# Hybrid decoder trunk: input projection as three fp32r products of parts, and a convolution by channel blocks

## The chip, the cores and the metric

The kernel runs on one core of a Trainium2 chip. The metric is the device time of one execution in microseconds, the median of the runs shown.

## What is computed

Two layers are applied to 576 tokens: a prompt of 512 (positions 0 to 511) and 8 sample sequences of 8 tokens. All arrays are float32, the model width is 1024. Each layer:

```python
a = rmsnorm(h, w['norm_mix'][i])
zaq, zaf, zai, zag, zbqkv, zbg, zbb, zba, zc, zd = split_in(a @ w['w_in'][i])
oA, sa = mixer_hgrn2(...)      # gated linear recurrence
oB, sb, bb = mixer_gdn(...)    # gated delta rule, after a causal 4-tap convolution
oC, bc = mixer_conformer(...)  # below
oD, bd = mixer_pool(...)       # means over windows of 2, 4, 8, 16 tokens
h += concat[oA | oB | oC | oD] @ W_out
h += PEER(rmsnorm(h))          # 8 heads, top 16 of 128 x 128 experts
h += sigmoid(rmsnorm(h) @ W_gate) * (p[i] @ W_ple)
```

The two parts that the change touches are the product `a @ w_in` and the depthwise convolution of the conformer mixer, 31 taps over 256 channels:

```python
a, b = jnp.split(zc, 2, axis=-1)
u = a * jax.nn.sigmoid(b)
y, new_buf = causal_dwconv(u, buf, dw_w)      # 31 taps
y = jax.nn.silu(layernorm(y + dw_b, ln_g, ln_b))
```

## The kernel before

Each engine has its own hand-written program (`@block.tensor`, `@block.scalar`, `@block.gpsimd`, `@block.vector`, `@block.sync`), and its instructions run in the order in which they are written; `at(label)` gives the semaphore value at which a named step is done. So each engine's queue is a list, and what stands behind a waiting instruction waits too.

At the start of a layer `rms` (ACT), `scale` (DVE), `turn` (PE) and `turned` (DVE, line 2197) put the normalised tokens transposed into XT, 128 features by 576 tokens for each of 8 blocks k; five token tiles i, the last being the samples. The input projection then makes 20 feature tiles of 128 output columns (`FM`, line 101): ca0, cb0, ca1, cb1 for the convolution, p0, p1 for the pooling, f0, f1, q0, q1, then k0 to k5, ga0, ga1, gb0, gb1. A tile is done in two halves of 288 tokens, "p" and "s", 8 float32 products each (`feature_half`, line 829), so that the first halves can begin before the last tokens are there; the trace shows each float32 product as two records. Its weights, 512 KB, come into a ring of three buffers WF, loaded by SyncE when the tile three before it is done (line 655). After tiles 0 to 9 comes a token-major tile of 264 columns ("zt", line 880). Tiles 10 to 19 are mixed with other work of the mixers on PE.

ACT drains each half (`take`, line 1595), except ca0 and ca1: their drain is the gate on DVE (line 2268), which multiplies the PSUM half with the sigmoid into CU. When both channel blocks c are gated, DVE runs the convolution: for each of the 31 taps j, for both blocks c, one instruction for the 512 prompt tokens and one for the 64 sample tokens:

```python
for j in range(CCONV):
    for c in range(2):
        ...
        dve.did(STT(out, src, w, out, ALU.mult, ALU.add) ...)   # line 2282
    dve.wait_ge(dve_done, count("dve_done"))
```

Behind it stand, in DVE's queue, the pooling sums (lines 2297 to 2309), the forget gate (2318 to 2321), the scans (2333), the convolution's mean and variance (2345, 2360), and the memset of HSP (2373), after which POOL zeroes QP and KLOW (2056, 2057) and ACT copies into QP (1680). Then the score loop: 16 units u of the HGRN2 mixer. DVE makes the exponent's argument (`decay_steps`, 2390), ACT the exponentials (`unit_exp`, 1687 and 1688), POOL `k_low` (2066), DVE `q_low` (2400), PE the scores (`pair_scores`, 921), and DVE chooses them (`chosen`, 2412); every second unit DVE also runs one block of the 4-tap convolution (`conv`, 2448). PE does one feature tile per two units.

The later query projection (`query_half`, line 1339) is already written as three products of parts: a high part is an ACT copy into fp32r, a low part is a subtraction.

Of the kernel before, what the change touches and what calls it, by code (L numbers as in the profile page):

```python
# [23 lines left out]
D = 1024  # L24
# [168 lines left out]
def trunk(nc, din, dout, gates_dram, gelus_dram, known):  # L193
# [145 lines left out]
    AM = region(RING, 4, 128)  # L339
    place["at"] = QR_AT  # L340
# [99 lines left out]
    phase.close()  # L440

# [364 lines left out]
    def _(eng):  # L806
        pe = Engine(eng, "pe_done", counts)
        mm = eng.matmul

# [53 lines left out]
        for L in range(DEPTH):  # L863
# [10 lines left out]
            pe.wait_ge(sem("wt_loaded"), at("wt", L))  # L874
            for i in range(NT):
# [3 lines left out]
                for k in range(KT):  # L879
                    ins = mm(b[0:R, 0:TMW], XT[:, k, COL[i]:COL[i] + R], WT[:, k, :], start=(k == 0), stop=(k == KT - 1))  # L880
# [447 lines left out]
            PARTS = ((0, 0), (1, 0), (0, 1))  # L1328

# [224 lines left out]
    def _(eng):  # L1554
# [71 lines left out]

        act.wait_ge(sem("const_loaded"), at("consts"))
        for L in range(DEPTH):
            if L == 0:
                for i in range(NT):  # L1630
                    rms(0, i)
            if L:

                act.wait_ge(dve_done, at("lbx", L))
                act.did(A(LBV[:, 6:10], LBV[:, 6:10], ACT.Exp).then_inc(act_done, 1), "lbe", L)
            for j in range(FM_FIRST):
                take(L, j)
            for i in range(NT):
# [12 lines left out]
            take(L, FM_FIRST)  # L1651
            act.wait_ge(dve_done, at("cyc", L))
# [7 lines left out]
            take(L, FM_FIRST + 1)  # L1660
            act.wait_ge(dve_done, at("hla", L))
# [368 lines left out]
            sigmoid(3, 0)  # L2030
            sigmoid(3, 1)
            rms(3 * L + 3, 3)
            sigmoid(SAMPLE, 0)
            sigmoid(SAMPLE, 1)
            rms(3 * L + 3, SAMPLE)


    @block.gpsimd
    def _(eng):
        pool = Engine(eng, "pool_done", counts)  # L2040

        for L in range(DEPTH):

            if L:
                pool.wait_ge(dve_done, at("ple_done", L - 1))
# [9 lines left out]
            pool.wait_ge(dve_done, at("temps_free", L))  # L2055
# [122 lines left out]
    def _(eng):  # L2178
# [48 lines left out]

        dve.wait_ge(sem("const_loaded"), at("consts"))
        dve.wait_ge(sem("params_loaded"), at("params", 0))
        lg = par("logits")  # L2230
        for L in range(DEPTH):
            if L == 0:
                for i in range(NT):
                    scale(0, i)
                    if i:
                        turned(0, i - 1)
            turned(3 * L, NT - 1)

# [21 lines left out]
            for c in range(2):  # L2260
# [8 lines left out]
                counts.same(("cu_ready", L, c), ("drained", "z", L, ja, "s"))  # L2269
            for c in range(2):  # L2270
                dve.wait_ge(sem(f"cu{c}_loaded"), at("cu", L, c))
            dve.wait_ge(dve_done, count("dve_done"))

            for j in range(CCONV):
                for c in range(2):
                    w = par("cconv")[:, c * CCONV + j:c * CCONV + j + 1]
                    for out, src in ((CY[:, c, 0:SEQ], CU[:, c, j:j + SEQ]),
# [743 lines left out]
```

## Time and profile before

| | |
|---|---|
| median of 3 runs | 3974.62 us |
| the runs | 3991.79, 3974.62, 3974.47 us |
| span of the profiled execution | 3986.0 us |
| its mean granted TensorE clock | 0.981 of full speed |
| busy: PE, DVE, ACT, POOL | 3860.7, 2869.4, 1527.8, 2356.9 us |

The profiled execution's own time isn't listed apart; the span lies between two of the runs, so only the run of 3991.79 us can be its. Busy time is the time in which an engine executes. "Idle before" is the gap on the engine ahead of an instruction, with what ended it. PE is the matmul side of TensorE, PEld its weight loads.

### The profile page before, as it was taken

The page shows a single profiled execution, that of the slowest core. Times are in us where ns is not written, and L with a number is a line of the kernel's source. Part 1 is how long each engine was busy: PE and PEld are TensorE (multiplying, and loading weights), DVE is VectorE, ACT ScalarE, POOL GpSimd, SP SyncE. Part 2 cuts the span into 40 slices and gives each one's busy share as a digit, 9 for nine tenths or more (in the row PEclk, how much of TensorE's full clock was granted, in tenths as well). Part 3 has the DMA queues.
Part 4 walks back from the last instruction along what each step waited for, and adds up shares of the span by engine and source line. Part 5 has one row for each costly group of instructions (what it writes and reads, how often), then busy time and mean ns, then how long its engine had stood idle before and what let it go on. Part 6 is the DMA issues. An engine that isn't in the chain of part 4 may idle for free.

```text
span 3986.0 us, 59450 instructions
## 1 busy us (share of the span) xinstructions
PE 3860.7 (97%) x23204; PEld 3451.3 (87%) x23204; DVE 2869.4 (72%) x4845; ACT 1527.8 (38%) x2347; POOL 2356.9 (59%) x1456
## 2 busy tenths in 40 slices
PE   8999999999999999999999999999999999999999
PEld 6788699998999999999477876999999999999994
DVE  5765369945888778888467642799458887788875
ACT  1443255543333343333314422555433333343333
POOL 0131088887777568888101410888877774788881
PEclk9989999999999999999999889999999999999999
DMA  4201156666989999999221021566579999999992
GB/s 122 53 13 70 48 184 214 214 218 232 313 308 324 339 347 367 384 371 350 86 66 40 13 75 53 187 223 209 206 252 321 312 322 334 351 376 379 375 321 71
DMA packets 417976, 900.99 MB, mean 226 GB/s; under 512 B 94497, under 2 KB 242209, under 8 KB 416033
## 3 DMA queue, kind: packets, MB, share of 16 engines
q1 hardware_dynamic: 272288, 552.91, 40.6%
q0 software_dynamic: 90112, 268.76, 18.7%
q10 hardware_dynamic: 55296, 75.52, 5.2%
q8 instruction: 184, 3.01, 0.3%
q14 instruction: 96, 0.78, 0.1%
HBM read 773.87 MB, written 123.15 MB: 225 GB/s over the span
## 4 chain that ended last, share of the span: by engine, by line
PE 50%; POOL 23%; DVE 12%; DMA 7%; issue 6%; ACT 2%; DVEq 0%; SPq 0%; ACTq 0%; POOLq 0%
PE banks L1410 14%; POOL peer_gates L2128 10%; POOL u_stage L2144 9%; PE banks L839 7%; PE banks L1422 6%; PE banks L1519 4%; POOL u_stage L2136 3%; DMA peer_gates<-peer_v,u_stage 3%; PE banks L1321 3%; PE banks L1339 3%; DMA u_stage<-peer_ut 2%; DVE normed L2796 2%; PE banks L1484 2%; PE banks L1465 1%; DMA normed<-peer_ut 1%
## 5 line engine op out<-in xcount | busy, mean ns | idle before, releaser
L2128 POOL DMA_INDIRECT peer_gates<-peer_v,u_stage x512 | 778.7, 1521 | 323.7 <-DVE normed L2796 151.9
L1484 PE MATMUL banks<-gated_parts,v_parts 128*128 128x320 f32 x6144 | 916.1, 310 | 44.3 <-DVE gated_parts L2843 33.8
L1484 PEld LDWEIGHTS banks<-gated_parts,v_parts 128*128 128x128 f32 x6144 | 904.1, 188 | 56.6 <-issue 55.8
L1410 PE MATMUL banks<-peer_x_parts,u_parts 128*128 128x448 f32 x3168 | 662.9, 367 | 0.0
L1410 PEld LDWEIGHTS banks<-peer_x_parts,u_parts 128*128 128x128 f32 x3168 | 591.0, 188 | 44.8
L2144 POOL DMA_INDIRECT u_stage<-dense_gelus,u_stage x256 | 418.9, 1636 | 103.8 <-issue 77.4
L2812 DVE SCALAR_TENSOR_TENSOR peer_gates<-peer_gates,u_stage 128x1024 f32<-128x1024 f32 x254 | 326.0, 1283 | 150.0 <-DMA peer_gates<-peer_v,u_stage 138.1
L1410 PE MATMUL banks<-peer_x_parts,low_s 128*128 128x448 f32 x1696 | 397.7, 367 | 0.0
L2796 DVE SCALAR_TENSOR_TENSOR normed<-peer_gates,u_stage,normed 128x1024 f32<-128x1024 f32 x254 | 327.6, 1290 | 89.3 <-DMA peer_gates<-peer_v,u_stage 62.5
L1915 ACT ACTIVATE u_stage<-banks 128x448 f32<-128x448 f32 x256 | 139.2, 544 | 633.5 <-PE banks L1410 506.8
L2121 POOL TENSOR_TENSOR parts_a<-x,parts_a 128x1024 fp32r<-128x1024 f32 x64 | 170.2, 2679 | 358.2 <-ACT parts_a L1864 358.2
L2136 POOL DMA_INDIRECT u_stage<-gelus,u_stage x256 | 332.2, 1298 | 78.2 <-issue 78.0
L1410 PEld LDWEIGHTS banks<-peer_x_parts,low_s 128*128 128x128 f32 x1696 | 317.3, 188 | 23.5
L1991 ACT ACTIVATE gated_parts<-gated 128x320 fp32r<-128x320 f32 x256 | 120.8, 472 | 562.7 <-DVE gated L2833 402.1
L2835 DVE TENSOR_TENSOR v_parts<-v_stage,v_parts 128x1024 fp32r<-128x1024 f32 x256 | 312.0, 1219 | 15.6 <-ACT v_parts L1989 11.0
L839 PE MATMUL banks<-x,mixers 128*128 128x288 f32 x1280 | 316.2, 408 | 1.3 <-DVE kept L2240 0.7
L839 PEld LDWEIGHTS banks<-x,mixers 128*128 128x128 f32 x1280 | 242.0, 190 | 68.3 <-issue 1.1
L1989 ACT ACTIVATE v_parts<-v_stage 128x1024 fp32r<-128x1024 f32 x256 | 267.9, 1046 | 19.9 <-PE banks L1484 12.7
L2782 DVE TENSOR_TENSOR u_parts<-u_stage,u_parts 128x1024 fp32r<-128x1024 f32 x114 | 137.6, 1220 | 84.8 <-ACT u_parts L1864 56.9
L2121 POOL TENSOR_TENSOR low_s<-u_stage,high_n 128x1024 fp32r<-128x1024 f32 x64 | 172.0, 2709 | 31.9 <-ACT high_n L1864 31.9
L2121 POOL TENSOR_TENSOR u_parts<-u_raw,u_parts 128x1024 fp32r<-128x1024 f32 x64 | 174.1, 2743 | 13.1 <-ACT u_parts L1864 13.1
L1465 PEld LDWEIGHTS banks<-x 128*128 128x128 f32 x1280 | 159.5, 197 | 22.3 <-DVE x L2776 20.3
(364 smaller groups left out, 6611.8 us busy)
## 6 DMA issues: line engine op xcount, KB each, us to landing
v_stage<-peer_v SPq DMA_DIRECT2D x256, 512.0 KB
u_stage<-peer_ut SPq DMA_DIRECT2D x244, 512.0 KB, 5.2
dense_gelus<-u_stage ACTq DMA_DIRECT2D x256, 224.0 KB
gates<-peer_gates SPq DMA_DIRECT2D x16, 2560.0 KB
u_stage<-gates SPq DMA_DIRECT2D x64, 640.0 KB
gated<-dense_gelus SPq DMA_DIRECT2D x256, 160.0 KB
x<-peer_ut SPq DMA_DIRECT2D x64, 512.0 KB, 4.6
u_raw<-peer_ut SPq DMA_DIRECT2D x64, 512.0 KB, 5.0
```

Source lines behind the costliest of these rows:

```text
L839: ins = mm(b[:, 0:c1 - c0], w[:, k * 128:(k + 1) * 128], XT[:, k, c0:c1], start=(k == 0), stop=(k == KT - 1))
L1410: ins = mm(PS[:, d % 2, 0:DW], u_part(n, a, k), XR[:, b, k, DENSE0:TOK], start=(k == 0 and m == 0), stop=(k == KT - 1 and m == 2))
L1422: ins = mm(PS[:, 2 + p % 2, 0:256].rearrange("p (r e) -> p r e", r=2), XR[:, b, k, 0:DENSE0], both[a][:, :, k * 128:(k + 1) * 128], start= ...
L1484: ins = mm(vc[k][:, 0:PW3], VR[:, s, b, k * 128:(k + 1) * 128], HR[:, s, a, :], start=(j == 0 and m == 0), stop=(j == NKEYS - 1 and m == 2))
L1989: A(VR[:, s, 0, :], VS[:, s, :], ACT.Copy).then_inc(v_hi, 1)
L2121: eng.tensor_tensor(low, raw, high.bitcast(F32), ALU.subtract).then_inc(u_low, 1)
L2128: eng.indirect_dma_start(out=GU[:, t % 4, :], out_offset=None, in_=din["peer_v"].rearrange("l i j d -> (l i j) d"), in_offset=bass.Indirec ...
L2136: eng.indirect_dma_start(out=WGTG[:, m:m + 1], out_offset=None, in_=natural_dram.rearrange("p (e o) -> (p e) o", o=1), in_offset=bass.Indi ...
L2144: eng.indirect_dma_start(out=WGT[:, s:s + 1], out_offset=None, in_=dense_dram.rearrange("i j (t o) -> (i j t) o", o=1), in_offset=bass.Ind ...
L2796: ins = STT(XN[:, 0, :], GU[:, m % 4, :], w, XN[:, 0, :], ALU.mult, ALU.add)
L2812: ins = STT(PICKSUM, GU[:, t % 4, :], w, PICKSUM, ALU.mult, ALU.add)
L2835: TT(VR[:, s, 1, :], VS[:, s, :], VR[:, s, 0, :].bitcast(F32), ALU.subtract).then_inc(v_low, 1)
```

## The change

Both layers, four edits.

1. Tokens and weights of the projection are split into a high part (rounded to fp32r) and a low part (the rest). `x_high(L, i)` and `wf_high(L, j)` are ACT copies into XH and into three high-weight buffers; `x_low` and `wf_low` are subtractions that write over XT and WF in place. `wf_low` runs on POOL; `x_low` runs on DVE in layer 0 and for the samples, on POOL for the other tiles of layer 1. The token-major weights get `wt_high` on ACT and `wt_low` on POOL. The product of a half becomes three fp32r products per k.
2. The convolution runs block by block: gate block 0, its taps 0 to 15, gate block 1, its taps 16 to 30, then the 31 taps of block 1. Each tap waits for the instruction before the last, not for all.
3. POOL zeroes QP and KLOW after waiting for the mixers' outputs itself; HSP is zeroed on DVE behind the score loop.
4. Buffers move: CQ and ST lie in MIXT's place, XH takes the end of the temporaries, HSP goes behind AM.

```diff
         def feature_half(L, j, part):
-            pe.wait_ge(sem(f"wf{j % NWF}_loaded"), at("wf", L, j))
-            w = WF[:, j % NWF, :]
+            pe.wait_ge(pool_done, at("wf_low", L, j))
+            w = (wf_high_at(j), WFL[:, j % NWF, :])
             for i in range(3) if part == "p" else range(NT):
-                pe.wait_ge(dve_done, at("drained", "xt", 3 * L, i, 1))
+                pe.wait_ge(*made("x_low", L, i))
             for k in range(KT):
-                ins = mm(b[:, 0:c1 - c0], w[:, k * 128:(k + 1) * 128], XT[:, k, c0:c1],
-                         start=(k == 0), stop=(k == KT - 1))
+                for n, (wp, xp) in enumerate(PARTS):
+                    ins = mm(b[:, 0:c1 - c0], w[wp][:, k * 128:(k + 1) * 128], (XH, XL)[xp][:, k, c0:c1],
+                             start=(k == 0 and n == 0), stop=(k == KT - 1 and n == 2))
...
+        def x_high(L, i):      # ACT
+            act.wait_ge(dve_done, at("drained", "xt", 3 * L, i, 1))
+            act.did(A(XH[:, :, cols], XT[:, :, cols], ACT.Copy) ..., "x_high", L, i)
+        def wf_high(L, j):
+            if j >= 2:
+                act.wait_ge(pe_done, at("fm", L, j - 2))
+            act.wait_ge(sem(f"wf{j % NWF}_loaded"), at("wf", L, j))
+            act.did(A(wf_high_at(j), WF[:, j % NWF, :], ACT.Copy) ..., "wf_high", L, j)
...
             for j in range(FM_FIRST):
                 take(L, j)
+                wf_high(L, j + 2)
+                if j == 4:
+                    act.did(A(WTH, WT, ACT.Copy) ..., "wt_high", L)
...
             take(L, FM_FIRST + 2)
+            wf_high(L, FM_FIRST + 4)
             for p in range(HUNITS // 2):
                 if FM_FIRST + 3 + p < NFM:
                     take(L, FM_FIRST + 3 + p)
+                    wf_high(L, FM_FIRST + 5 + p)
...
+        def wf_low(L, j):      # POOL
+            pool.wait_ge(act_done, at("wf_high", L, j))
+            pool.did(eng.tensor_tensor(WFL[:, j % NWF, :], WF[:, j % NWF, :], wf_high_at(j).bitcast(F32), ALU.subtract) ...)
...
-            pool.wait_ge(dve_done, at("temps_free", L))
+            for j in range(0 if L == 0 else 2, FM_FIRST + 4):
+                wf_low(L, j)
+                if j == 6:
+                    pool.did(eng.tensor_tensor(WTL, WT, WTH.bitcast(F32), ALU.subtract) ..., "wt_low", L)
+            pool.wait_ge(act_done, at("cout", L))
             pool.did(eng.memset(QP, 0.0) ..., "q_zero", L)
...
             for u in range(2, HUNITS):
+                if u % 2 == 0 and FM_FIRST + 3 + u // 2 < NFM:
+                    wf_low(L, FM_FIRST + 3 + u // 2)
...
+            gated_rows(0)
             for c in range(2):
                 dve.wait_ge(sem(f"cu{c}_loaded"), at("cu", L, c))
-            dve.wait_ge(dve_done, count("dve_done"))
-            for j in range(CCONV):
-                for c in range(2):
+                dve.wait_ge(dve_done, at("cu_ready", L, c))
+                for j in range(CCONV):
...
+                            dve.wait_ge(dve_done, count("dve_done") - 1)
                             dve.did(STT(out, src, w, out, ALU.mult, ALU.add) ...)
-                dve.wait_ge(dve_done, count("dve_done"))
+                    if (c, j) == (0, CCONV // 2):
+                        gated_rows(1)
```

How instructions move on two queues, in layer 0. POOL before, from the last of the border memsets to the first `k_low` (L2066; `mixers` is the large block of buffers that holds WF, QP, KF and the rest):

```order
L2052 MEMSET mixers 64x8
L2056 MEMSET mixers 128x2304
L2057 MEMSET mixers 128x1152
L2066 ISA
L2066 TENSOR_TENSOR mixers<-mixers 128x288 x2
```

POOL now, from `wf_low(4)` to `k_low(7)` (L2126 is `wf_low`, L2160 `wt_low`, L2177 `k_low`; `high_el`, `high_la` and the second `w_parts` hold high parts of weights):

```order
L2126 TENSOR_TENSOR w_parts<-mixers,high_el 128x1024 x3
L2160 TENSOR_TENSOR w_parts<-mixers,high_la 128x2112
L2126 TENSOR_TENSOR w_parts<-mixers,high_el 128x1024 x5
L2126 TENSOR_TENSOR w_parts<-mixers,w_parts 128x1024 x2
L2165 MEMSET mixers 128x2304
L2166 MEMSET mixers 128x1152
L2126 TENSOR_TENSOR w_parts<-mixers,w_parts 128x1024
L2177 TENSOR_TENSOR mixers<-mixers 128x288 x2
L2126 TENSOR_TENSOR w_parts<-mixers,w_parts 128x1024
L2177 TENSOR_TENSOR mixers<-mixers 128x144x2 x2
```

POOL had nothing between the border memsets and the zeroing of QP; now 14 `wf_low` and `wt_low` stand there, and one `wf_low` ahead of each pair of `k_low` after it, six in all.

DVE before, where the convolution begins (L2268 the gates, L2280 tap 0, L2282 the others):

```order
L2268 TENSOR_TENSOR mixers<-banks,mixers 128x288
L2268 TENSOR_TENSOR mixers<-banks,mixers 128x224
L2268 TENSOR_TENSOR mixers<-banks,mixers 128x8x8
L2268 TENSOR_TENSOR mixers<-banks,mixers 128x288
L2268 TENSOR_TENSOR mixers<-banks,mixers 128x224
L2268 TENSOR_TENSOR mixers<-banks,mixers 128x8x8
L2280 TENSOR_SCALAR mixers<-mixers,kept 128x512
L2280 TENSOR_SCALAR mixers<-mixers,kept 128x64
```

DVE now, at the same place (L2343 `x_low` of the samples, L2391 the gates of block 0, L2403 and L2406 its taps):

```order
L2343 TENSOR_TENSOR x_low<-x,x_high 128x8x64
L2361 MEMSET kept 128x2
L2363 TENSOR_SCALAR kept<-kept 128x2
L2391 TENSOR_TENSOR mixers<-banks,mixers 128x288
L2391 TENSOR_TENSOR mixers<-banks,mixers 128x224
L2391 TENSOR_TENSOR mixers<-banks,mixers 128x8x8
L2403 TENSOR_SCALAR mixers<-mixers,kept 128x512
L2403 TENSOR_SCALAR mixers<-mixers,kept 128x64
L2406 SCALAR_TENSOR_TENSOR mixers<-mixers,kept 128x512
L2406 SCALAR_TENSOR_TENSOR mixers<-mixers,kept 128x64
```

The taps of block 0 now follow its own gates; those of block 1 stand behind tap 15 of block 0.

## Rows read from the trace of the kernel before

**Rows 1.** The page, part 1: busy us, share of the span and instructions of each engine.

```profile
PE 3860.7 (97%) x23204; PEld 3451.3 (87%) x23204; DVE 2869.4 (72%) x4845; ACT 1527.8 (38%) x2347; POOL 2356.9 (59%) x1456
```

**Rows 2.** The chain in order of time, layer 0's projection: start us, us, what.

```profile
32.75 70.08 PE banks L839 x288
102.83 17.94 PE banks L880 x80
...
132.94 7.97 PE banks L839 x32
```

**Rows 3.** Timeline of DVE, layer 0: start us, us, instruction, count, [idle before, releaser].

```profile
57.41 1.45 DVE L2280 TENSOR_SCALAR mixers<-mixers,kept 128x512 f32<-128x512 f32 x4
58.90 55.23 DVE L2282 SCALAR_TENSOR_TENSOR mixers<-mixers,kept 128x512 f32<-128x512 f32 x120
...
142.49 1.36 DVE L2355 TENSOR_TENSOR mixers<-mixers 128x1152 f32<-128x1152 f32 x1 [8.35 <-ACT mixers L1662]
...
164.54 1.57 DVE L2400 TENSOR_TENSOR mixers<-mixers 64x288 f32<-64x288 f32 x2 [1.42 <-ACT mixers L1688]
...
168.22 2.92 DVE L2448 SCALAR_TENSOR_TENSOR mixers<-mixers,kept 128x512 f32<-128x512 f32 x6
...
182.23 0.75 DVE L2390 TENSOR_TENSOR mixers<-mixers 128x576 f32<-128x576 f32 x1
...
191.62 0.69 DVE L2390 TENSOR_TENSOR mixers<-mixers 128x512 f32<-128x512 f32 x1
...
221.42 0.69 DVE L2390 TENSOR_TENSOR mixers<-mixers 128x512 f32<-128x512 f32 x1
```

**Rows 4.** The same timeline in layer 1: the convolution's first tap, the pooling's first sum.

```profile
2036.27 1.45 DVE L2280 TENSOR_SCALAR mixers<-mixers,kept 128x512 f32<-128x512 f32 x4
...
2093.03 0.71 DVE L2297 TENSOR_TENSOR mixers<-mixers 128x526 f32<-128x526 f32 x1
```

**Rows 5.** The chain in order of time, query projection in three products of parts.

```profile
462.94 47.92 PE banks L1339 x360
```

**Rows 6.** Lines that make parts: count, duration ns min/median/max, first and last start us.

```profile
L1837 ACT ACTIVATE u_parts<-peer_scores x16: 1046/1059/1062, 395.4 to 2484.2; 128x1024 fp32r<-128x1024 f32 x16
L2636 DVE TENSOR_TENSOR u_parts<-peer_scores,u_parts x16: 1210/1226/1226, 398.3 to 2485.3; 128x1024 fp32r<-128x1024 f32 x16
L2121 POOL TENSOR_TENSOR parts_a<-x,parts_a x64: 2351/2408/4460, 502.8 to 2859.3; 128x1024 fp32r<-128x1024 f32 x64
```

**Rows 7.** Timeline of ACT and PE at the start: end of rms(2), first feature products.

```profile
17.72 0.29 ACT L1571 ACTIVATE kept<-kept 128x1 f32<-128x1 f32 x1
...
22.87 8.55 PE L839 MATMUL banks<-x,mixers 128*128 128x288 f32 x32
```

**Rows 8.** DMA issues of weight tiles: count, KB each, median us to landing.

```profile
mixers<-w_fm SPq DMA_DIRECT2D x40, 512.0 KB, 3.5
```

**Rows 9.** Timeline of POOL, layer 0.

```profile
156.05 2.02 POOL L2056 MEMSET mixers<- 128x2304 f32 x1 [154.68 <-DVE normed L2375]
```

**Rows 10.** DVE and POOL side by side, timelines, and one line's durations in ns.

```profile
719.31 4.41 DVE L2728 TENSOR_TENSOR peer_scores<-peer_scores,kept 128x2048 f32<-128x2048 f32 x1
...
728.17 2.29 DVE L2732 TENSOR_REDUCE peer_scores<-peer_scores 128x128 f32<-128x2048 f32 x1
...
721.51 8.84 POOL L2121 TENSOR_TENSOR u_parts<-u_raw,u_parts 128x1024 fp32r<-128x1024 f32 x2
...
893.34 3.42 DVE L2774 TENSOR_TENSOR x<-kept,u_stage 128x1024 f32<-128x1024 f32 x1
...
892.77 2.91 POOL L2121 TENSOR_TENSOR u_parts<-u_raw,u_parts 128x1024 fp32r<-128x1024 f32 x1 [0.69 <-ACT u_parts L1864]
...
L2400 DVE TENSOR_TENSOR mixers<-mixers x56: 390/445/1184, 164.5 to 2206.6; 64x256 f32<-64x256 f32 x32, 64x288 f32<-64x288 f32 x24
```

**Rows 11.** Timeline of ACT, the copies into QP.

```profile
158.10 2.80 ACT L1680 ACTIVATE mixers<-mixers 64x576 f32<-64x576 f32 x4 [2.41 <-POOL mixers L2056]
```

**Rows 12.** A stretch with gaps on PE: busy us of PE, PEld, DVE, ACT, POOL, granted clock, DMA.

```profile
227.00:240.00 13.00, 11.27 (x75) 10.70 (x74) 9.10 (x24) 7.79 (x16) 9.50 (x9) 0.71 0.09 32
```

More of the change, by code:

```diff
@@ L339, in trunk @@
     AM = region(RING, 4, 128)
+    HSP = region(5, 2, 128)
+    assert XH_AT <= TMP + 9815 and place["at"] <= TMP + TMPW
     place["at"] = QR_AT
@@ L440, in trunk, with wf_high_at @@
     phase.close()
+    phase = ExitStack()
+    memory(phase, "normed_gap", 2 * D)
+    memory(phase, "x_low", KT * TOK, F32R)
+    XL = region(KT, TOK)
+    memory(phase, "mixed_gap", WFbase)
+    memory(phase, "w_parts", NWF * D + KT * TMW, F32R)
+    WFL = region(NWF, D)
+    WTL = region(KT, TMW)
+    place["at"] = NWF * D
+    HIGH_WT = region(2, D)
+    memory(phase, "zq_kf_gap", 2 * 2 * TOK)
+    memory(phase, "high_la", 2 * 2 * TOK, F32R)
+    HIGH_LA = region(D)
+    place["at"] = 0
+    WTH = region(KT, TMW)
+    memory(phase, "lf_gap", 2 * TOK)
+    memory(phase, "high_el", 2 * 2 * TOK, F32R)
+    HIGH_EL = region(D)
+    place["at"] = 2 * TOK
+    HIGH_GA = region(D)
+    memory(phase, "mixers_gap", XH_AT - (Wbase + 7 * 2 * TOK))
+    memory(phase, "x_high", KT * TOK, F32R)
+    XH = region(KT, TOK)
+    phase.close()
+    def wf_high_at(j):
+        if j >= FM_FIRST + 2:
+            return HIGH_WT[:, j % 2]
+        return HIGH_EL if j % 2 == 0 else HIGH_LA if j < 4 else HIGH_GA
     def const(name):
@@ L1629, in _ @@
             if L == 0:
-                for i in range(NT):
+                for i in range(3):
                     rms(0, i)
+                x_high(0, 0)
+                rms(0, 3)
+                wf_high(0, 0)
+                x_high(0, 1)
+                rms(0, SAMPLE)
+                x_high(0, 2)
+                wf_high(0, 1)
+                x_high(0, 3)
+            x_high(L, SAMPLE)
             if L:
@@ L1637, in _ @@
                 take(L, j)
+                wf_high(L, j + 2)
+                if j == 4:
+                    act.wait_ge(sem("wt_loaded"), at("wt", L))
+                    act.did(A(WTH, WT, ACT.Copy).then_inc(act_done, 1), "wt_high", L)
             for i in range(NT):
@@ L2030, in _ @@
             sigmoid(3, 0)
+            if L + 1 < DEPTH:
+                x_high(L + 1, 0)
+                wf_high(L + 1, 0)
             sigmoid(3, 1)
             rms(3 * L + 3, 3)
+            if L + 1 < DEPTH:
+                x_high(L + 1, 1)
+                wf_high(L + 1, 1)
             sigmoid(SAMPLE, 0)
+            if L + 1 < DEPTH:
+                x_high(L + 1, 2)
             sigmoid(SAMPLE, 1)
             rms(3 * L + 3, SAMPLE)
+            if L + 1 < DEPTH:
+                x_high(L + 1, 3)
     @block.gpsimd
@@ L2040, in _, with x_low @@
         pool = Engine(eng, "pool_done", counts)
+        def wf_low(L, j):
+            pool.wait_ge(act_done, at("wf_high", L, j))
+            pool.did(eng.tensor_tensor(WFL[:, j % NWF, :], WF[:, j % NWF, :], wf_high_at(j).bitcast(F32), ALU.subtract)
+                     .then_inc(pool_done, 1), "wf_low", L, j)
+        def x_low(L, i):
+            cols = slice(COL[i], COL[i] + ROWS[i])
+            pool.wait_ge(act_done, at("x_high", L, i))
+            pool.did(eng.tensor_tensor(XL[:, :, cols], XT[:, :, cols], XH[:, :, cols].bitcast(F32), ALU.subtract)
+                     .then_inc(pool_done, 1), "x_low", L, i)
         for L in range(DEPTH):
             if L:
+                x_low(L, 0)
+                wf_low(L, 0)
+                x_low(L, 1)
+                wf_low(L, 1)
+                x_low(L, 2)
+                x_low(L, 3)
                 pool.wait_ge(dve_done, at("ple_done", L - 1))
@@ L2225, in add_h, with x_low @@
                 counts.same(("h", u, i), ("drained", label, L, i, half))
+        def x_low(L, i):
+            cols = slice(COL[i], COL[i] + ROWS[i])
+            dve.wait_ge(act_done, at("x_high", L, i))
+            dve.did(TT(XL[:, :, cols], XT[:, :, cols], XH[:, :, cols].bitcast(F32), ALU.subtract).then_inc(dve_done, 1), "x_low", L, i)
         dve.wait_ge(sem("const_loaded"), at("consts"))
@@ L2372, in _ @@
             dve.wait_ge(sem("pool_stored"), at("pool_out", L, 1))
-            dve.did(eng.memset(HSP, 0.0).then_inc(dve_done, 1), "temps_free", L)
             dve.wait_ge(act_done, at("beta", L))
@@ L2491, in _ @@
             dve.wait_ge(pe_done, at("w_in", L))
+            dve.did(eng.memset(HSP, 0.0).then_inc(dve_done, 1), "hsp_zero", L)
             for c in range(2, 4):
```

45 lines of the change are left out of this document (34 added, 11 removed).

## Prediction

> **What bounds the kernel now.** I read the page's busy shares and chain first, then the chain in order of time, then the engines' timelines in the stretch that is edited. The page puts PE at 97% of the span [rows 1]. In order of time layer 0's projection (line 839) is one stretch without a gap: 288 records in 70.08 us, then the token-major tile in 17.94 us, and from 132.94 us on single tiles of 7.97 us, between which other work stands [rows 2]. So PE looks like the bound of all of it, and a faster product like a plain gain.
>
> DVE's timeline says something else. The 31-tap convolution starts at 57.41 us, when the fourth feature tile is drained, and runs without a gap to 58.90 + 55.23 = 114.13 us; the pooling and the forget gate stand behind it in the same queue, and the first long wait is one of 8.35 us at 142.49 us [rows 3]. From 160 us on both engines are nearly full. The score loop makes six turns (decays, chosen scores, one 4-tap convolution each) from 164.54 to 221.42 us; the one from 182.23 to 191.62 us, 9.4 us long, holds no wait of DVE [rows 3]; PE's tile and two sets of scores fill most of the same time. So in the edited stretch there are two chains of about equal length, and the question is what the edit does to DVE's. Layer 1 repeats the pattern: its convolution runs from 2036.27 to 2093.03 us [rows 4].
>
> **The products on PE.** The kernel already has the new form in its query projection: 360 records in 47.92 us is 133 ns each, so a tile of 48 takes 6.39 us [rows 5] instead of 7.97 us. The token-major tile becomes 120 records of 264 columns; at no more than 133 ns that is under 16 us instead of 17.94; I take 14.5. Tiles 0 to 9 and this tile thus end some 16 us sooner after their start. That is a gain only if DVE follows.
>
> **The start.** Parts have to exist before the first product. The copies cost 1.06 us each on ACT and 1.23 us on DVE for 128x1024 [rows 6]; the subtraction on POOL takes 2.41 us [rows 6]. In layer 0 the feature tiles start at 22.87 us, after the third turned tile; ACT ends rms(2) at 18.0 us [rows 7]. Behind it now stand three x_high and one wf_high of 1.06 us and two rms of 1.5 us (a square as long as a copy, and a root), to 25.3 us, and x_low(2) on DVE: 26.5 us. Two first halves (3.2 us each), the sample's turn and drain as before (1.5 us) and its half-width copy and subtraction (0.65 us each, half of [rows 6] and a little) lead to 36.3 us for the second halves, which started at 32.75 [rows 2]: 3.6 us later. In layer 1 x_low goes to POOL, which then has nothing else to do; it is ready in time, and by the same steps the restart moves by 0.5 us. Weight tiles land 3.5 us after their issue [rows 8], against 6.4 us a tile, so the DMA stays hidden, as do wf_high (1.06) and wf_low (2.41) behind PE's tile.
>
> **The convolution's start.** Channel block 0 needs only tiles 0 and 1. With second halves at 36.3 us (one stall of 0.6 us for wf_low(2) is behind that point) and 6.4 us for a tile, plus the gate's 0.9 us, it starts at 43.8 us instead of 57.41: 13.6 us earlier. In layer 1, from 2012.1 us, it starts at 2020.3 us instead of 2036.27: 16.0 us earlier. Its own work hardly changes: 62 pairs took 56.7 us, 0.92 us each; the new waits are like those of the 4-tap convolution, 3 pairs in 2.92 us [rows 3], 0.97. Between these ends I take 0.93, and 1.0 us for block 1's gates, which now stand inside: +1.9 us.
>
> **What the subtractions do to DVE.** This decides. Before the change POOL is idle for 154.68 us up to its memset at 156.05 us [rows 9]. Now it runs one wf_low per tile while DVE convolves. The rows show that these two don't overlap freely. DVE's TENSOR_TENSOR L2774, with both inputs of 1024 columns in SBUF, takes 3.42 us, where one of that shape takes 1.23 [rows 6, 10]; just then POOL subtracts, and takes 2.91 instead of 2.41. At 719.31 us DVE's L2728, of 2048 columns, takes 4.41 us and two POOL subtractions take 8.84 instead of 4.8 [rows 10]: each waits for whole instructions of the other. The TENSOR_REDUCE behind it, over as many columns but with one input, takes 2.29 us beside a POOL subtraction. Inside the mixer L2400 takes up to 1.18 us beside k_low, with a median of 0.45 [rows 10]. So one subtraction costs DVE 3.42 - 1.23 = 2.2 or 4.41 - 2.29 = 2.1 us. The convolution is SCALAR_TENSOR_TENSOR, of which no row shows one beside POOL; its two inputs CU and CY are both in SBUF, so I take the same 2.2 us. Bounds: 0 (this form is exempt) and 2.41 (the whole subtraction).
>
> The Trainium skill (SBUF — State Buffer, "Who interferes with whom") makes no exception for the form: a DVE instruction with two SBUF inputs contends with a GpSimd instruction that reads SBUF, and the loser blocks for the whole instruction. By that rule the sum is the one below; if it did not hold for this form, the first rival's.
>
> PE's tiles don't depend on DVE, so wf_low(3) to wf_low(11) all fall into the convolution, and wt_low with them: 9 x 2.2 us, and 4.7 us for 2112 columns, 24.5 us. Convolution's end: -13.6 + 1.9 + 24.5 = +12.8 us in layer 0, and -16.0 + 1.9 + 24.5 = +10.4 in layer 1.
>
> **From there to the scores.** ACT no longer waits for tile 11, which PE ended at 140.9 us [rows 2], since ACT now comes later: 2.4 us of DVE's 8.35 go. wf_low(13) falls on L2355 and costs 1.7 (2.2 less a wait of 0.5 that it covers). QP's zeroing hangs on cout itself, no longer on DVE's memset and its queue: the copies into QP at 158.10 us, which waited 2.41 us for POOL [rows 11], come that much sooner. Together -3.1. Two wf_high stand ahead of the first exponentials: +2.1. The six turns: without any wait DVE needs 6.5 us for the rest of the first (164.54 to 171.1), 9.4 for each of three, and about 8.7 for two whose units cover 512 instead of 576 columns, 52.1 for what took 56.9 [rows 3]: -4.8; wf_low(15) to (19) each fall in one, partly under chosen(), which reads PSUM: between 1.3 and 2.2 us each, I take 1.7, +8.5. The HSP memset of 1280 columns moves to the end (POOL's of 2304 takes 2.02 us [rows 9]); half hidden, +0.5. PE now stands idle 8 to 11 us twice while DVE finishes. Where PE has gaps, as in 227 to 240 us, the granted clock is 0.71 [rows 12], part of it at the level of 1.2 GHz: 3.8 us of work less in 13 us. I count 1.7 once per layer, between 0 and 5.
>
> Sum: layer 0 12.8 - 3.1 + 2.1 - 4.8 + 8.5 + 0.5 + 1.7 = +17.7; layer 1 2.4 less, +15.3; **+33.0 us**. The profiled execution spans 3986.0 us; of the runs shown only that of 3991.79 us can hold it, so about 4025 us for one like it. The other two stand 17 us lower and carry the median; I put the difference on it: 3974.6 + 33.0 = **4007.6 us**. Both layers' later stretches are untouched.
>
> **Rivals.** *SCALAR_TENSOR_TENSOR is not blocked.* Then per layer 24.5 + 1.7 + 8.5 us and the clock's 1.7 go, 72.8 in all: -39.8 us, 3935 us. For it: nothing in the trace shows this form slowed, and without a block the start of the convolution, 14 to 16 us earlier, reaches the end nearly whole. Against it: the rows slow every TENSOR_TENSOR with two SBUF inputs and none with one. It decides from a block of 1.15 us per subtraction: below that the change wins. 18%.
>
> *A half block.* The subtraction is blocked rather than DVE, or each costs DVE only some 1.2 us, because POOL waits its turn behind several short taps. Then the 34.7 us per layer shrink to 19, the sum is +1.4, 3976 us. POOL would show subtractions of 4 us and more; the rows, where the two alternate strictly, speak against it. 18%.
>
> *PE stalls on the parts.* POOL, slowed by up to 0.75 us per wf_low and with wt_low (5 us) between two tiles, delivers late and PE waits. wf_low(7) would be ready 0.2 us ahead of its tile. Even with 2 us per tile PE ends zt before the convolution, so only the start would move: +5 us on the forecast, 4013 us; it is inside the forecast's range and shares its 64%.
>
> **How the numbers follow.** The forecast holds 64%. Its own range, with 2.1 to 2.41 us per subtraction in the convolution and 1.3 to 2.2 in the turns, the start 2 us off either way and the clock's 0 to 5, is 3993 to 4027. The range for 8 in 10 reaches over the half block down to 3953, leaving out nearly all of the first rival (16%) and 4% above: 3953 to 4028. 0.5% of the time is 20 us, about what a measurement of this kernel can tell from no change. Slower than 3994.5: nine tenths of the forecast (0.58) and a little of the half block (0.02), 0.60. Within 0.5%: the rest of the forecast (0.05, where a term is missing) and most of the half block (0.14), 0.19. Faster: the first rival and a little of the half block, 0.21.
>
> **What would show it.** Right: the convolution starts near 44 us and ends near 127, with a dozen taps of 2.5 us and more; wf_low takes 2.4 to 3.2 us; PE is idle behind tile 10 for about 10 us; tiles take 6.4 us. The score turns take 11 us each. Wrong: no tap over 0.8 us and an end near 102 us (first rival), or POOL subtractions of 4 us beside an end near 115 us (half block); or the first feature product much later than 26.5 us.

## Result, and the profile after

| | median of 20 runs | profiled span | TensorE busy | VectorE busy | clock |
|---|---|---|---|---|---|
| before | 3974.34 us (3948.95 to 4009.85) | 3986.0 us | 3860.7 us | 2869.4 us | 0.981 |
| after | 3999.38 us (3974.67 to 4025.88) | 3993.2 us | 3819.1 us | 2931.5 us | 0.975 |

The changed kernel takes 1.0055 times as long, 95% interval 1.0035 to 1.0075: about 22 us slower (14 to 30); the medians differ by 25. The forecast was +33. TensorE works 42 us less over the whole program than in [rows 1], and the program is slower all the same. The page of the changed kernel, parts 1 and 5:

```profile
PE 3819.1 (96%) x23924; PEld 3480.9 (87%) x23924; DVE 2931.5 (73%) x4851; ACT 1583.1 (40%) x2399; POOL 2393.9 (60%) x1502
L878 PE MATMUL banks<-x_high,w_parts 128*128 128x288 f32 x896 | 226.0, 307 | 1.3 <-POOL w_parts L2126 1.2
```

VectorE's timeline in layer 0 (start us, us, instruction, count, [idle before, releaser]), which answers to [rows 3]:

```profile
21.81 2.91 DVE L2299 TENSOR_SCALAR normed<-kept 128x1024 f32<-128x1024 f32 x1
...
29.02 3.58 DVE L2343 TENSOR_TENSOR x_low<-x,x_high 128x1024 fp32r<-128x1024 f32 x2
...
52.77 2.85 DVE L2403 TENSOR_SCALAR mixers<-mixers,kept 128x512 f32<-128x512 f32 x2
...
73.51 27.87 DVE L2406 SCALAR_TENSOR_TENSOR mixers<-mixers,kept 128x512 f32<-128x512 f32 x30
...
101.99 28.00 DVE L2406 SCALAR_TENSOR_TENSOR mixers<-mixers,kept 128x512 f32<-128x512 f32 x60
130.02 0.71 DVE L2423 TENSOR_TENSOR mixers<-mixers 128x526 f32<-128x526 f32 x1
...
157.53 2.61 DVE L2481 TENSOR_TENSOR mixers<-mixers 128x1152 f32<-128x1152 f32 x1 [5.37 <-ACT mixers L1731]
...
182.54 2.18 DVE L2569 TENSOR_SCALAR mixers<-mixers,kept 128x512 f32<-128x512 f32 x2
...
193.46 2.52 DVE L2569 TENSOR_SCALAR mixers<-mixers,kept 128x512 f32<-128x512 f32 x2
```

The convolution starts 4.6 us sooner than in [rows 3], at 52.77 us, and ends 15.9 us later, at 130.0. A tap of one block is two instructions here, one of 512 columns and one of 64. The thirty instructions from 73.51 us last as long as the sixty from 101.99. A window on one instant shows a single record: an instruction of 64 columns that meets no subtraction, and one that does.

```profile
64.36 0.27 DVE L2406 SCALAR_TENSOR_TENSOR mixers<-mixers,kept 128x64 f32<-128x64 f32 x1
```

```profile
60.50 2.42 DVE L2406 SCALAR_TENSOR_TENSOR mixers<-mixers,kept 128x64 f32<-128x64 f32 x1
```

GpSimd in the same stretch, where [rows 9] had an idle time of 154.68 us:

```profile
53.13 2.43 POOL L2126 TENSOR_TENSOR w_parts<-mixers,high_la 128x1024 fp32r<-128x1024 f32 x1 [1.11 <-ACT high_la L1679]
59.89 2.94 POOL L2126 TENSOR_TENSOR w_parts<-mixers,high_el 128x1024 fp32r<-128x1024 f32 x1 [4.32 <-ACT high_el L1679]
66.56 2.70 POOL L2126 TENSOR_TENSOR w_parts<-mixers,high_el 128x1024 fp32r<-128x1024 f32 x1 [3.73 <-ACT high_el L1679]
73.00 2.40 POOL L2126 TENSOR_TENSOR w_parts<-mixers,high_el 128x1024 fp32r<-128x1024 f32 x1 [3.73 <-ACT high_el L1679]
75.37 5.20 POOL L2160 TENSOR_TENSOR w_parts<-mixers,high_la 128x2112 fp32r<-128x2112 f32 x1
```

There is one such row about every 6.4 us, and beside each an instruction of the convolution of 2.4 us or a little more (beside the first row it is the TENSOR_SCALAR of tap 0); beside L2160 there is one of 4.78. The subtractions that start while an instruction of 512 columns runs (0.74 us) are themselves 0.3 to 0.5 us longer (2.70, 2.94): they wait that one out, and the next one waits for them.

**Where the 25 us arise.** The same points in the traces of both kernels, in us (the last column is the difference):

| | before | after | |
|---|---|---|---|
| layer 0: first tap | 57.4 | 52.8 | -4.6 |
| layer 0: last tap ends | 114.1 | 130.0 | +15.9 |
| layer 0: query projection starts | 458.9 | 477.0 | +18.1 |
| layer 1: first feature product | 2002.4 | 2015.3 | +12.9 |
| layer 1: first tap | 2036.3 | 2032.3 | -4.0 |
| layer 1: last tap ends | 2093.0 | 2109.6 | +16.6 |
| layer 1: query projection starts | 2443.4 | 2462.7 | +19.3 |

The edited stretches add 18.1 us in layer 0 and 19.3 - 12.9 = 6.4 in layer 1, together 24.5, close to the 25.0 between the medians. The two spans differ by 7.2 only, because the stretches without an edit vary: from the query projection of layer 0 to the first feature product of layer 1 the trace before has 1543.5 us, this one 1538.3, and the eight kernels below 1524.8 to 1545.3; behind the query projection of layer 1 the trace before has 1542.6 us and this one 1530.5. Single runs of one kernel spread over 50 us and more. So the points of a trace ahead of the query projection tell a few us, single times do not.

### The profile page after: what moved, and what is told of

It reads as the page before. It is cut to its first block, busy times and chain, and to the rows that moved or that the text cites. A ratio compares the mean times of both kernels' runs of the same rounds, so it can differ in the third digit from the quotient of the medians.

```text
span 3993.2 us, 61006 instructions
## 1 busy us (share of the span) xinstructions
PE 3819.1 (96%) x23924; PEld 3480.9 (87%) x23924; DVE 2931.5 (73%) x4851; ACT 1583.1 (40%) x2399; POOL 2393.9 (60%) x1502
## 4 chain that ended last, share of the span: by engine, by line
PE 48%; POOL 16%; DVE 16%; DMA 12%; issue 6%; ACT 2%; another core or an unknown queue 0%; SPq 0%; DVEq 0%; ACTq 0%; POOLq 0%
PE banks L1449 17%; PE banks L1461 8%; POOL peer_gates L2239 7%; POOL u_stage L2255 5%; DMA u_stage<-peer_ut 4%; DVE mixers L2406 4%; PE banks L1558 4%; DMA peer_gates<-peer_v,u_stage 3%; PE banks L1362 3%; PE banks L1378 3%; DMA gated<-dense_gelus 3%; POOL u_stage L2247 2%; DVE normed L2921 2%; PE banks L1523 2%; PE banks L1504 1%
## 5 line engine op out<-in xcount | busy, mean ns | idle before, releaser
L2239 POOL DMA_INDIRECT peer_gates<-peer_v,u_stage x512 | 740.7, 1447 | 387.1 <-DVE normed L2921 163.2
L2255 POOL DMA_INDIRECT u_stage<-dense_gelus,u_stage x256 | 381.9, 1492 | 105.5 <-issue 77.5
L2921 DVE SCALAR_TENSOR_TENSOR normed<-peer_gates,u_stage,normed 128x1024 f32<-128x1024 f32 x254 | 327.6, 1290 | 77.1 <-DMA peer_gates<-peer_v,u_stage 57.4
L878 PE MATMUL banks<-x_high,w_parts 128*128 128x288 f32 x896 | 226.0, 307 | 1.3 <-POOL w_parts L2126 1.2
L2232 POOL TENSOR_TENSOR low_s<-u_stage,high_n 128x1024 fp32r<-128x1024 f32 x64 | 181.4, 2856 | 39.1 <-ACT high_n L1935 39.1
L2232 POOL TENSOR_TENSOR low_s<-u_stage,high_c 128x1024 fp32r<-128x1024 f32 x64 | 168.8, 2659 | 21.8 <-ACT high_c L1935 21.8
L2898 DVE TENSOR_TENSOR x<-kept,u_stage 128x1024 f32<-128x1024 f32 x80 | 101.6, 1270 | 102.4 <-PE banks L1449 102.4
```

The source lines that it names most:

```text
L878: ins = mm(b[:, 0:c1 - c0], w[wp][:, k * 128:(k + 1) * 128], (XH, XL)[xp][:, k, c0:c1], start=(k == 0 and n == 0), stop=(k == KT - 1 and n ...
L2232: eng.tensor_tensor(low, raw, high.bitcast(F32), ALU.subtract).then_inc(u_low, 1)
L2239: eng.indirect_dma_start(out=GU[:, t % 4, :], out_offset=None, in_=din["peer_v"].rearrange("l i j d -> (l i j) d"), in_offset=bass.Indirec ...
L2255: eng.indirect_dma_start(out=WGT[:, s:s + 1], out_offset=None, in_=dense_dram.rearrange("i j (t o) -> (i j t) o", o=1), in_offset=bass.Ind ...
L2921: ins = STT(XN[:, 0, :], GU[:, m % 4, :], w, XN[:, 0, :], ALU.mult, ALU.add)
```

## The experiments

Eight more kernels ran. Ratios are to runs of the kernel before made beside them: 11 for blocks_only, parts_only, low_memset and low_on_dve (median 3977.2 us), 23 for the other four (median 3966.5 us). So compare ratios and not medians across the two groups. Theory: a GpSimd subtraction holds a VectorE instruction with both inputs in SBUF, the memory on the chip that both engines work in, for its whole length, and without this the change would win. Rivals: the new order of the convolution costs; the parts cost elsewhere (copies, start); any GpSimd work holds VectorE.

### One part alone: blocks_only and parts_only

blocks_only is the kernel before with this in its convolution:

```diff
+            gated_rows(0)
             for c in range(2):
                 dve.wait_ge(sem(f"cu{c}_loaded"), at("cu", L, c))
-            dve.wait_ge(dve_done, count("dve_done"))
-
-            for j in range(CCONV):
-                for c in range(2):
+                dve.wait_ge(dve_done, at("cu_ready", L, c))
+                for j in range(CCONV):
...
+                            dve.wait_ge(dve_done, count("dve_done") - 1)
                             dve.did(STT(out, src, w, out, ALU.mult, ALU.add) ...)
-                dve.wait_ge(dve_done, count("dve_done"))
+                    if (c, j) == (0, CCONV // 2):
+                        gated_rows(1)
+            dve.wait_ge(dve_done, count("dve_done"))
```

> The kernel before with the convolution by channel blocks alone (float32 products, no parts). The theory (a GpSimd subtraction holds a VectorE tap, the new order of the convolution itself is harmless): layer 0's convolution starts at 41.5 us instead of 57.4, has 0.86 us a pair as in the changed kernel, no tap over 0.8 us, and ends near 96 us. TensorE's tile 11 still ends near 139 us, so the wait of VectorE behind the forget gate grows from 8.35 us to some 20, and only 2 to 5 us per layer are left: 3974 - 4 to -10 us. The rival (the new order and its waits cost the time): as long as the changed kernel, 3990 us or more.

parts_only is the changed kernel with the reverse of that.

> The changed kernel with the convolution across both blocks again, as it was before; the products of parts and GpSimd's subtractions stay. The theory: layer 0's convolution starts near 65 us (tile 3 is drained two tiles of 6.4 us after the changed kernel's start of 52.8), takes its old 56.8 us and eight blocks, 7 x 2.2 + 4.7 = 20.1 us, and ends near 142 instead of 130 us; layer 1 ends 12 us later than the changed kernel too: 3999 + 24, about 4023 us. The rival (order costs, parts don't): 3974 us or less.

Measured: blocks_only 3979.0 us, ratio 1.0011 (0.9974 to 1.0049). parts_only 4026.2 us, ratio 1.0117 (1.0082 to 1.0152), the 4023 expected. Their convolutions, the first tap, other taps and the pooling's first sum, blocks_only and then parts_only:

```profile
42.70 0.77 DVE L2281 TENSOR_SCALAR mixers<-mixers,kept 128x512 f32<-128x512 f32 x2
...
71.57 25.84 DVE L2284 SCALAR_TENSOR_TENSOR mixers<-mixers,kept 128x512 f32<-128x512 f32 x60
97.45 0.71 DVE L2301 TENSOR_TENSOR mixers<-mixers 128x526 f32<-128x526 f32 x1
```

```profile
65.99 3.54 DVE L2402 TENSOR_SCALAR mixers<-mixers,kept 128x512 f32<-128x512 f32 x4
69.56 72.60 DVE L2404 SCALAR_TENSOR_TENSOR mixers<-mixers,kept 128x512 f32<-128x512 f32 x120
142.19 0.71 DVE L2419 TENSOR_TENSOR mixers<-mixers 128x526 f32<-128x526 f32 x1
```

The order alone lets the convolution end at 97.4 us, 16.7 sooner than before. The ratio's interval, -10 to +19 us, neither shows nor excludes the 4 to 10 us that were expected. The trace shows no gain: from the first feature product to the last decay of the score turns (L2390 and its like) layer 0 takes 202.2 us against 201.7 before, and layer 1 takes 201.0 in both. The chain of waits of blocks_only shows why: it runs on TensorE from tile to tile.

```profile
33.59 70.08 PE banks L839 x288
103.67 17.94 PE banks L880 x80
121.61 7.96 PE banks L839 x32
...
133.77 7.97 PE banks L839 x32
...
165.03 7.96 PE banks L839 x32
```

VectorE only waits longer, in two places instead of one:

```profile
122.12 0.18 DVE L2329 TENSOR_TENSOR normed<-mixers,kept 128x20 f32<-128x20 f32 x1 [11.67 <-ACT mixers L1643]
...
143.32 1.36 DVE L2359 TENSOR_TENSOR mixers<-mixers 128x1152 f32<-128x1152 f32 x1 [10.37 <-ACT mixers L1662]
```

So the order does no harm that shows (54.7 us against 56.7 of [rows 3], a pair every 0.86 us), and the parts with their subtractions cost 46 us (33 to 60), of which the order gives back some 25. Neither half pays alone. VectorE's and TensorE's chains are of about equal length, and the order starts VectorE's sooner while the parts shorten TensorE's.

### What on GpSimd holds VectorE: low_memset, low_copy, low_in_four

low_memset, with the same for `WTL`:

```diff
-            pool.did(eng.tensor_tensor(WFL[:, j % NWF, :], WF[:, j % NWF, :], wf_high_at(j).bitcast(F32), ALU.subtract)
-                     .then_inc(pool_done, 1), "wf_low", L, j)
+            for n in range(3):
+                pool.wait_ge(pool_done, count("pool_done"))
+                pool.did(eng.memset(WFL[:, j % NWF, :].bitcast(F32), 0.0).then_inc(pool_done, 1), *(("wf_low", L, j) if n == 2 else ()))
```

> The changed kernel with the low parts of the weights left out of the computation: GpSimd writes zeros into them, three memsets in place of each subtraction (2.7 us of 1024 columns, some 5.5 us of 2112), so it is as busy as before in the same places but reads nothing. The theory (it is GpSimd's reading of SBUF that holds VectorE): no tap over 0.8 us, the convolution of layer 0 takes 54 us instead of 77.2, the doubled scale at the start goes, the turns lose 1.9 us each; about -37 us on the kernel before, 3937 us. The rival (any GpSimd access to SBUF, or GpSimd being busy at all, holds VectorE): taps of 2.4 us beside the memsets as beside the subtractions, 3999 us. Between: memsets hold single taps for less, 3960 us.

Measured 3949.3 us, ratio 0.9937 (0.9903 to 0.9970), 28 us under the kernel before and, by the two ratios, some 47 under the changed one. It was expected 37 us under the kernel before. Part of what is missing may be the TENSOR_SCALARs below, which memsets hold too: a pair of them takes 1.7 to 2.1 us in the first five turns instead of 0.7. GpSimd and VectorE side by side, then the first line of the 4-tap convolution (count, ns min/median/max, first and last start):

```profile
64.27 2.98 POOL L2128 MEMSET w_parts<- 128x1024 f32 x3 [3.69 <-ACT high_el L1679]
70.70 2.98 POOL L2128 MEMSET w_parts<- 128x1024 f32 x3 [3.45 <-ACT high_el L1679]
```

```profile
64.45 12.97 DVE L2409 SCALAR_TENSOR_TENSOR mixers<-mixers,kept 128x512 f32<-128x512 f32 x30
...
105.03 0.71 DVE L2426 TENSOR_TENSOR mixers<-mixers 128x526 f32<-128x526 f32 x1
```

```profile
L2572 DVE TENSOR_SCALAR mixers<-mixers,kept x24: 248/1017/1122, 161.1 to 2171.0; 128x512 f32<-128x512 f32 x12, 128x64 f32<-128x64 f32 x12
```

Thirty instructions of the taps beside these memsets take 12.97 us, as long as thirty beside none in blocks_only (12.96), and the convolution lasts 55.1 us. The one of 1.73 us in it stands behind a held TENSOR_SCALAR. So the rival that any GpSimd work holds the taps has fallen. But a TENSOR_SCALAR, with a single tensor as input, takes 1.02 us at the median beside memsets of 0.95 to 1.12, where all_low_on_dve (below) has 0.24 us for 64 columns and 0.48 for 512: that form is held by writing too.

low_copy replaces the subtraction by `eng.tensor_copy(WFL[:, j % NWF, :], WF[:, j % NWF, :])`, and low_in_four cuts it into four over 256 columns each.

> The changed kernel with a copy of the weights in place of each subtraction on GpSimd (so the low parts are wrong ones: the difference is left out of the computation). It has one input in SBUF where the subtraction has two. The theory (any reading by GpSimd holds a tap with two SBUF inputs for the whole instruction): taps beside a copy last as long as the copy, and the convolution of layer 0 takes 54 us plus the copies' sum. The rival (only two-input instructions of GpSimd hold it): no tap over 0.8 us and 54 us.

> The changed kernel with each subtraction of a weight tile on GpSimd cut into four of 256 columns. The theory (whole instructions hold each other, by turns): each piece holds one tap for its 0.6 us, four of them 2.4 us per tile as before, and GpSimd waits for taps in between, so its four pieces take 3.5 to 5 us in all; layer 0's convolution takes 77 us give or take 2. The rival (short pieces pass beside the taps): the convolution under 68 us.

Each ran once, 3955.5 and 3983.2 us, so only their traces count. low_copy's copies (CAST) take 1.08 us at the median, the 64 columns beside one of 1.05 us take 1.06, and its convolution lasts from 49.1 to 111.6 us, 62.5, between 54.7 without and 77.2 with subtractions. Reading one input is enough, and the price is the GpSimd instruction's length less what the held one would have taken by itself, 1.06 - 0.27 = 0.8 us. low_in_four's convolution lasts from 50.9 to 126.9 us, 76.0, as the theory had it. Its four pieces of one tile, and an instruction between them that waits for the second (0.74 us normally):

```profile
65.12 3.73 POOL L2128 TENSOR_TENSOR w_parts<-mixers,high_el 128x256 fp32r<-128x256 f32 x4 [3.39 <-ACT high_el L1679]
```

```profile
66.31 1.25 DVE L2408 SCALAR_TENSOR_TENSOR mixers<-mixers,kept 128x512 f32<-128x512 f32 x1
```

The pieces and the taps take turns, none runs beside the other, and cutting gains next to nothing (`wt_low` stayed whole).

### Is the rest of the parts free: memset_across

parts_only with the memsets of low_memset.

> parts_only with GpSimd's subtractions of weights replaced by memsets of about the same length, so the low parts of the weights are left out: convolution across both blocks, no reading by GpSimd. The theory: the whole of the 46 us between parts_only and the kernel before is the blocks. Layer 0's convolution starts near 63 us, takes its old 56.8 us and ends near 120 (before 114), layer 1's ends 5 us sooner than before relative to its start; with shorter turns 3977 - 0 to -15, about 3968 us, and some 20 us more than low_memset, since the convolution starts two tiles (12.8 us) later in each layer. The rival (the parts cost elsewhere too, the copies on ScalarE or the start): 3990 us or more.

Measured 3963.3 us, ratio 1.0000 (0.9979 to 1.0022), where 9 us under the kernel before were expected (3968 against 3977). Its convolution runs from 64.7 to 122.7 us. So the parts break even in the old order once no subtraction holds a tap. By ratios, the holds cost 1.0117 - 1.0000, 46 us, in the old order and 1.0055 - 0.9937, 47 us, in the new one; the new order is worth 25 us with the parts in either case, and without them nothing that shows. The ratios' intervals leave some 10 to 16 us either way on each of these differences.

### VectorE subtracts itself: low_on_dve and all_low_on_dve

```diff
+            wf_low(L, 2)
             gated_rows(0)
+            wf_low(L, 3)
+            LOWS = {8: 4, 14: 5, 20: 6, 26: 7, 30: 8, 35: 9, 41: 10, 48: 11}
...
+                    if CCONV * c + j in LOWS:
+                        wf_low(L, LOWS[CCONV * c + j])
```

> The changed kernel with layer 0's first subtractions and in both layers those of tiles 2 to 11 and of the token-major weights done by VectorE itself, between the taps (1.22 us each, 2.5 us for 2112 columns), the rest on GpSimd as before. The theory: VectorE does 13.5 us more work of its own and loses 23.3 us of blocks, so the convolution takes 67.4 us instead of 77.2, layer 0 starts 1 us sooner: 3999 - 21 = 3978 us. The rival (the blocks are not what makes the convolution longer, or a subtraction costs VectorE under 1.2 us): 3999 + up to 27 us, 4026 us.

> As low_on_dve, and VectorE also does the subtractions of tiles 12 to 19, which GpSimd did in the middle and in the score turns: those of tiles 12, 13 and 14 inside waits of VectorE, those of 15 to 19 ahead of each turn's 4-tap convolution. GpSimd then subtracts only the first parts of layer 1. The theory (a subtraction of 1.22 us on VectorE is cheaper than a block of 1.9): in the middle 2 us and in the turns 5 x 0.7 = 3.5 us less than low_on_dve per layer, 3984 - 11 = 3973 us, about the kernel before. It does not beat it clearly, since layer 0 still starts late. The rival (the turns are bound by TensorE or by ScalarE, not by VectorE): 3984 us, as low_on_dve.

Measured: low_on_dve 3984.1 us, ratio 1.0017 (0.9981 to 1.0052); its convolution lasts 65.1 us (67.4 expected). all_low_on_dve 3961.2 us, ratio 0.9995 (0.9973 to 1.0017). Both are level with the kernel before. Only the second is faster than the changed kernel clear of the noise; the first's interval overlaps 1.0035 to 1.0075. So 1.22 us of VectorE per tile, for 1.6 us of TensorE, is about the break-even here. Whether the second's further 11 us came stays open: by the ratios it is 9 us below the first with intervals that overlap, but in the traces it takes no less from the first feature product to the last decay (201.7 and 196.8 us in the two layers, against 199.1 and 196.7). No TENSOR_SCALAR of its turns is held any more,

```profile
L2579 DVE TENSOR_SCALAR mixers<-mixers,kept x24: 239/356/482, 169.3 to 2191.5; 128x512 f32<-128x512 f32 x12, 128x64 f32<-128x64 f32 x12
```

but TensorE gets a lower clock in the same stretch. Busy us of PE, PEld, DVE, ACT, POOL, granted clock and DMA, layer 0, all_low_on_dve and then low_on_dve:

```profile
165.00:240.00 75.00, 64.62 (x444) 62.41 (x442) 65.22 (x139) 37.66 (x69) 15.85 (x17) 0.88 0.18 30
```

```profile
165.00:240.00 75.00, 64.59 (x482) 61.78 (x480) 69.81 (x138) 40.58 (x71) 30.52 (x25) 0.97 0.20 30
```

The same busy time holds 444 products instead of 482, three of its tiles take 7.9 to 8.5 us instead of 6.4, and VectorE waits 6.6 us for scores where it had waited 1.2. That the clock alone is the cause is inferred, not isolated. No version that keeps the whole computation beat the kernel before.

## Why the prediction was right, and which terms were off

The sign, the mechanism and the forecast case held; measured +22 by the ratio (14 to 30) and +25 by the medians against +33, at 3999.4 us inside the forecast's own range of 3993 to 4027. The first two rivals fell: instructions of 2.4 us rule out the first, and the half block's subtractions of 4 us and its end near 115 us are not there. It was worth saying that both inputs lie in SBUF: that the form is no exception was an inference from TENSOR_TENSOR rows [rows 10], and the traces of after, low_memset and low_copy bear it out. The Trainium skill (SBUF — State Buffer, "Who interferes with whom") says the same in finer terms: a two-input VectorE instruction meets a GpSimd instruction that reads SBUF, not one that only writes. The traces agree: thirty instructions of the taps take 12.97 us beside memsets and 12.96 beside none, and one beside a copy of 1.05 us takes 1.06 instead of 0.27.

- **What the subtractions do to DVE**: 24.5 us per layer forecast; 77.2 - 54.7 = 22.5 measured in both layers. One term of the sum, right to a tenth.
- **The start**: first product forecast at 26.5 us, measured at 31.6; convolution at 43.8, measured 52.77, +9.0. This step failed in layer 0. The sum counted blocks only in the convolution and forgot that POOL's first two subtractions fall beside DVE's own work there: the scale of tile 3 takes 2.91 us instead of 0.75 and one x_low 2.44 instead of 1.22. Both stand ahead of the first product, so they are 3.4 of its 5.1 us; in low_memset, where that x_low takes 1.21 and the scale 1.49, it comes at 29.4. The other 1.7 us are a chain longer than the sum had it. (The terms given for the second halves also add up to 35.7 us and not 36.3.) And the first products run at half pace, below. In layer 1 the start is right: -4.0 - 12.9 = -16.9 against -16.0.
- **Its own work hardly changes, +1.9 us**: mis-sized in sign. The waits inside a block are for the instruction before the last and cost nothing in the trace, and the pause of 0.1 us at the end of each tap across both blocks goes: 54.7 us with block 1's gates inside (blocks_only) instead of 56.7, so -2.0. This made both layers 3.9 us better than forecast. With the 2.0 of the subtractions it offset 5.9 of the start's 9.0 us in layer 0: +15.9 for +12.8 there, and 16.6 - 12.9 = +3.7 for +10.4 in layer 1.
- **The middle**, -3.1 and +2.1: the first turn's low queries start at 179.53 us, +15.0, so -0.9 for -1.0.
- **The turns**, -4.8 + 8.5: layer 0 measures +2.3 for +3.7. The five blocks are 1.5 to 2.1 us each, 9.3 us in all (8.5 forecast), but on another instruction than expected: all five fall on L2569, a TENSOR_SCALAR, and none on the two-tensor taps or the low queries. The clock and the HSP memset, 2.2 us in the forecast, weren't measured apart; 0.8 us are left for them.
- **Both layers**: +18.1 for +17.7, and +6.4 for +15.3. Layer 0's agreement is partly luck: a start 9.0 us later than forecast meets terms that were some 8.7 us too dear (3.9, 2.0, 1.4 of the turns, 1.4 of clock and memset). The 8.9 us of layer 1 are 6.7 at the convolution's end (0.9 start, 3.9 own work, 2.0 blocks), and a net 2.2 behind it, most of it in the untouched solve after the turns, where six of nine kernels come out 4 to 6 us ahead of the trace before; why, no run tells.
- **The third rival, PE stalls on the parts**: up to 110 us TensorE waits for a weight's subtraction once, for 0.4 us. Tiles take 6.4 us and the turns with a subtraction beside them 10.3 to 11.2, as forecast; behind tile 10 TensorE waits twice for VectorE, 5.8 us (line 932) and 6.5 us (line 945), 12.3 where I said 10.
- **Break-even at a block of 1.15 us**: three runs lie near it. With 1.22 us per tile on DVE the ratio is 1.0017 and 0.9995; with copies, which cost a tap 0.8 us each, the single run took 3955.5 us beside a median of 3966.5. They fit the break-even and don't prove it.

## What to carry to other kernels

Before moving work to an idle GpSimd, ask what VectorE does in that moment: if its instructions read two tensors from SBUF, a GpSimd instruction there that reads SBUF costs VectorE nearly its whole length (2.15 of 2.4 us here), and a TENSOR_SCALAR is held even by one that only writes. The same subtraction on VectorE itself took half of that (1.22 us). When two engines' chains are equally long, try an edit's parts alone and together: here the order was worth nothing that shows by itself and 25 us beside the parts. And compare points of the trace ahead of the stretches that vary, since 25 us is half of what single runs of this kernel spread.

## What the runs showed of the hardware that was not expected

**A form with one input is held too.** The prediction read the rows as "none with one", which was wrong for TENSOR_SCALAR. TENSOR_SCALAR of 512 and 64 columns takes 2.2 to 2.9 us as a pair beside a subtraction instead of 0.64 to 0.77, one of 1024 columns 2.91 instead of 0.75, and one of 64 columns beside a mere memset 1.02 instead of 0.24. The gates (TENSOR_TENSOR with one input in PSUM, the memory that TensorE writes), which run beside the subtraction at 73.00 us, keep their 0.87 us for three. The Trainium skill (SBUF — State Buffer, "Who interferes with whom") lists tensor_scalar among the forms whose fast mode takes the port pair shared with GpSimd; the traces agree.

**TensorE begins its products at the lower clock, and the clock's row can miss it.** The first parts' products, behind 4.86 us of idle time, come every 0.24 us until 37.2 us, then every 0.13:

```profile
31.60 0.58 PE L878 MATMUL banks<-x_high,high_el 128*128 128x288 f32 x1 [4.86 <-DVE x_low L2343]
31.98 0.44 PE L878 MATMUL banks<-x_high,w_parts 128*128 128x288 f32 x1
32.22 0.44 PE L878 MATMUL banks<-x_low,high_el 128*128 128x288 f32 x1
```

288 columns in 0.24 us are 1.2 columns per ns, the pace of the lower level, 1.2 GHz. The granted clock's row reads 1.00 there. Same columns as above:

```profile
31.50:37.20 5.70, 5.60 (x23) 5.63 (x24) 1.09 (x1) 0.00 (x0) 0.00 (x0) 1.00 0.00 0
37.20:43.40 6.20, 4.23 (x35) 3.93 (x33) 1.46 (x4) 0.63 (x1) 0.00 (x0) 1.00 0.00 0
43.40:47.40 4.00, 3.89 (x19) 3.92 (x20) 0.17 (x1) 0.00 (x0) 0.00 (x0) 0.60 0.02 4
```

That is a hole in the record: this trace's first record of the clock is at 37.4 us, and the view counts time without a record as 1.00. parts_only's records begin at 19.1 us. Its first products come every 0.24 us as well, and its row reads 0.50 (in the trace after, the row of 43.4 us, behind a pause of 2.1 us, shows the lower level too, with 0.60):

```profile
32.40:36.20 3.80, 3.72 (x15) 3.75 (x16) 1.07 (x1) 0.00 (x0) 0.00 (x0) 0.50 0.00 0
```

Nor did the idle time of 4.86 us bring the clock down. The eight transposes ahead of it were slow already (first row, after), where eight of the kernel before took little more than half as long (second row):

```profile
24.77 1.97 PE L863 MATMUL banks<-kept,normed 128*128 128x128 f32 x8 [3.38 <-DVE normed L2299]
```

```profile
19.05 1.10 PE L825 MATMUL banks<-kept,normed 128*128 128x128 f32 x8 [1.26 <-DVE normed L2188]
```

In the chain in order of time, the two stretches of 48 records that should take 6.4 us each:

```profile
31.60 9.18 PE banks L878 x48
...
43.51 8.17 PE banks L878 x48
```

That is 2.8 and 1.8 us, half of the 9.0 us by which layer 0's convolution started later than forecast. The kernel before had 8.55 us for its first 32 records, which followed the last turned tile without a pause [rows 7], and 7.97 for later ones: its row reads 0.50 only up to 24.1 us, 1.2 us behind its first product. So layer 0's late start has two parts: the first product comes later, and TensorE is slower for longer behind it.
